# Second layer's values with tokens on the partitions, two head pairs to a group, in a fused two-block transformer kernel

## The reference

```python
proj = x @ w_in                       # 2048 x 7680
aq, ak, av, ag, bq, bk, bv, bg, cu, cglu, cg = jnp.split(proj, IN_OFFSETS, axis=-1)
# a: 4 heads, differential attention: softmax(q1 k1) - lam * softmax(q2 k2), halves of 64
ya = diff_attention(aq, ak, av, ...) * jax.nn.silu(ag)
# b: 8 heads of 128, three dilated window patterns merged
yb = dilated_attention(bq, bk, bv, ...) * jax.nn.silu(bg)
# c: 512 channels, GLU, causal depthwise conv of 31 taps, layer norm, swish, pointwise
yc = conformer_conv(cu, cglu, ...) * jax.nn.silu(cg)
x = layer_norm(ALPHA * x + jnp.concatenate([ya, yb, yc], -1) @ w_out, ln_g, ln_b)
```

## Time and profile before

| | |
|---|---|
| time, median of 3 runs | 2912.65 us (2910.31 to 2913.6) |
| the profiled execution's own time | 2911.83 us |
| its span | 2910.0 us |
| TensorE busy | 2887.2 us, 99% of the span |
| VectorE, ScalarE, GpSimd busy | 71%, 47%, 14% |
| granted TensorE clock, mean | 0.999 of full speed |
| `dil`, `diffa`, `diffb` of the first layer | about 2024.8 to 2327.4 us of the span |
| the same of the second layer | about 2501.4 to 2803.9 us |

### The profile page before, as it was taken

One profiled execution on the slowest core, in us unless ns is written; L12 is line 12 of the kernel. 1 busy time (PEld: TensorE's weight loads), 2 busy tenths in 40 slices (PEclk: granted clock), 3 DMA queues, 4 the chain that ended last, 5 costly groups with the idle time before them and its releaser, 6 DMA issues.

```text
span 2910.0 us, 43427 instructions
## 1 busy us (share of the span) xinstructions
PE 2887.2 (99%) x16142; PEld 2498.9 (86%) x16142; DVE 2071.8 (71%) x2314; ACT 1362.9 (47%) x1618; POOL 419.0 (14%) x392
## 2 busy tenths in 40 slices
PE   9999999999999999999999999999999999999999
PEld 7888888888888888888888888888888888888887
DVE  6666667875687677765666667876887856788766
ACT  6554544346654444443343344544344545444453
POOL 1000000204020000000000000013950100891010
PEclk9999999999999999999999999999999999999999
DMA  6555565654465666666555565566555555555455
GB/s 217 174 173 166 159 186 186 210 159 143 126 195 188 187 199 202 189 190 192 174 180 188 188 194 185 175 194 192 168 174 165 159 194 153 175 174 173 157 177 174
DMA packets 479573, 520.58 MB, mean 179 GB/s; under 512 B 17720, under 2 KB 438699, under 8 KB 479176
## 3 DMA queue, kind: packets, MB, share of 16 engines
q1 hardware_dynamic: 474528, 509.68, 55.8%
q0 software_dynamic: 4080, 6.30, 0.8%
q10 hardware_dynamic: 824, 2.69, 0.3%
HBM read 516.49 MB, written 2.12 MB: 178 GB/s over the span
## 4 chain that ended last, share of the span: by engine, by line
PE 63%; DVE 6%; ACT 3%; issue 2%; DMA 0%; DVEq 0%; ACTq 0%; SPq 0%
PE PG L2104 37%; PE PG L2107 18%; DVE WL L1266 2%; PE PG L2136 2%; PE PG L2138 2%; PE PG L2137 2%; ACT WH L650 1%; DVE G L1279 1%; DVE G L1583 0%; DVE MIX L1700 0%; PE PX L2168 0%; PE PX L2320 0%; PE PX L2221 0%; PE PX L2157 0%; DMA RAW<-in_w_in_dram 0%
## 5 line engine op out<-in xcount | busy, mean ns | idle before, releaser
L1266 DVE TENSOR_TENSOR WL<-RAW,WH 128x1024 fp32r<-128x1024 f32 (+1 forms) x956 | 1150.4, 1232 | 501.6 <-ACT WH L650 488.0
L650 ACT ACTIVATE WH<-RAW 128x1024 fp32r<-128x1024 f32 (+1 forms) x972 | 997.8, 1050 | 786.8 <-PE PG L2107 456.5
L2104 PE MATMUL PG<-XH,WH 128*128 128x512 f32 x4096 | 1295.8, 398 | 8.3 <-DVE WL L1266 4.4
L2107 PEld LDWEIGHTS PG<-XH,WL 128*128 128x128 f32 x4096 | 770.2, 188 | 182.1
L2107 PE MATMUL PG<-XH,WL 128*128 128x256 f32 x4096 | 805.7, 278 | 0.0
L2104 PE MATMUL PG<-YH,WH 128*128 128x512 f32 x2336 | 736.0, 396 | 1.9 <-DVE WL L1266 1.9
L2104 PEld LDWEIGHTS PG<-XH,WH 128*128 128x128 f32 x4096 | 625.8, 189 | 15.2 <-issue 9.4
L2107 PEld LDWEIGHTS PG<-YH,WL 128*128 128x128 f32 x2336 | 438.8, 188 | 103.7
L2107 PE MATMUL PG<-YH,WL 128*128 128x256 f32 x2336 | 459.0, 278 | 0.0
L2104 PEld LDWEIGHTS PG<-YH,WH 128*128 128x128 f32 x2336 | 355.9, 189 | 5.3 <-issue 3.4
L1279 DVE TENSOR_REDUCE G<-PG 128x512 f32<-128x1024 f32 x174 | 212.0, 1218 | 33.9 <-PE PG L2107 33.8
(11 more groups left out here) (302 smaller groups left out, 2092.0 us busy)
## 6 DMA issues: line engine op xcount, KB each, us to landing
RAW<-in_w_in_dram SPq DMA_DIRECT2D x488, 512.0 KB, 4.6
RAW<-in_w_ffn_gu_dram SPq DMA_DIRECT2D x176, 512.0 KB, 4.6
RAW<-in_w_ffn_down_dram SPq DMA_DIRECT2D x88, 512.0 KB, 4.7
RAW<-in_w_out_dram SPq DMA_DIRECT2D x64, 512.0 KB, 4.6
RAW<-in_w_rnn_out_dram SPq DMA_DIRECT2D x40, 512.0 KB, 4.6
RAW<-in_w_attn_out_dram SPq DMA_DIRECT2D x32, 512.0 KB, 4.8
RAW<-in_w_o_dram SPq DMA_DIRECT2D x32, 512.0 KB, 4.8
RAW<-in_w_ple_gate_dram SPq DMA_DIRECT2D x32, 512.0 KB, 5.1
```

The source lines that it names most:

```text
L650: nc.scalar.activation(WH[:, u % SLOTS, 0:nk, :], RAW[:, u % SLOTS, 0:nk, :], ACT.Copy)\
L1266: V_.tensor_tensor(WL[:, u % SLOTS, 0:nk, :], RAW[:, u % SLOTS, 0:nk, :], WH[:, u % SLOTS, 0:nk, :].bitcast(fp), ALU.subtract).then_inc(s. ...
L2104: mm(PG[:, 2 * par + j, :], WH[:, slot, kk, P * j:P * j + P], x, start=grp.opens and n == 0 and kk == 0, stop=False)
L2107: last = mm(PG[:, 2 * par + j, T:2 * T], WL[:, slot, kk, P * j:P * j + P], x[:, 0:T], start=False, stop=grp.closes and n == len(units) - 1 ...
```

## The change

The values of the second block are computed by wide groups with tokens on the partitions: one wide group of 512 columns carries the values of two head pairs, so `dil` has two (one for each two pairs) and `diffa` has one, which also serves `diffb`. The four transposes of the values and their copy from PSUM are gone; VectorE copies the wide group's result from PSUM to V (`values`), and V moves to another part of SBUF. The loop over the pairs in `dil` is written out as two halves of seven groups (q, k, v wide, gate, q, k, gate). The order of the work is written out by hand for `dil` and `diffa` on all engines: `take(g, n)` splits a group's units up to n, `give(g, n)` splits the first n units of a coming group early. TensorE's attention steps now stand inside groups (a dictionary gives the unit after which each comes). In `diffb` the values group is gone, the gate follows the second half of the pointwise product, the scores stand after the gate's second unit, and the probabilities' transposes after the second unit of `outa`.

```diff
-        V = F[:, 2048:2560].rearrange("p (a n) -> p a n", a=4)
+        V = AL[:, 20 * 2 * T:22 * 2 * T].rearrange("p (b n) -> p b n", b=NB)
...
+            def part(o, m, wide=False, pool=()):
+                return Group(w2, DC, A0 + 512 * o + COLS * m, 0, XH, wide=wide, pool=pool)
-            phases.append(Phase(f"dil{l}", 4, [Group(w2, DC, B0 + 1024 * o, COLS, XH) for o in range(4)]))
+            dil = []
+            for i in range(2):
+                a, b = ([Group(w2, DC, B0 + 1024 * o + COLS * pair_, 0, XH) for o in (0, 1, 3)]
+                        for pair_ in (2 * i, 2 * i + 1))
+                v = Group(w2, DC, B0 + 2048 + 2 * COLS * i, 0, XH, wide=True)
+                dil += [a[0], a[1], v, a[2]] + b
+            phases.append(Phase(f"dil{l}", 1, dil))
+            phases.append(Phase(f"diffa{l}", 1, [part(0, 0), part(1, 0), part(2, 0, wide=True), part(3, 0)]))
+            phases.append(Phase(f"diffb{l}", 1, [part(0, 1), pw[0], part(1, 1), pw[1], part(3, 1, pool=range(4))],
...
-                    split_next(f"diffb{l}", 5, 1)
                     diff_high(0)
-                elif j == 4:
-                    evacuated()
+                    give([p for p in phases if p.name == f"outa{l}"][0].body[0], 2)
                     soft(4)
                 else:
...
-                V_.tensor_copy(V, PX[:, 2, :].rearrange("p (a n) -> p a n", a=4))
...
+            def values(grp):
+
+                par = c.n.get("group", 0) % 2
+                dve.wait_ge(s.unit, c.next("seen", grp.seen))
+                V_.tensor_copy(V, PG[:, 2 * par:2 * par + 2, :]).then_inc(s.evac, 1)
+                c.add("group")
+                dve.wait_ge(s.evac, c.value("group"))
+            def take(grp, n):
+                split(grp, slice(ahead[0], n))
+                ahead[0] = 0
+
+            def give(grp, n):
+                split(grp, slice(0, n))
+                ahead[0] = n
...
+            def dil(body, before, following, l):
+                for i in range(2):
+                    q0, k0, v, g0, q1, k1, g1 = body[7 * i:7 * i + 7]
+                    take(q0, 4)
+                    if i:
+                        gate(body[6])
+                        taps(7, 1, l)
+                        give(k0, 2)
+                        transposed()
+                    else:
+                        for job in before:
+                            job()
+                    take(k0, 4)
+                    evacuate(q0, two(QR[:, 0, :]))
+                    taps(8 * i, 1, l)
+                    give(v, 2)
+                    if i:
+                        dil_out(1)
+                    take(v, 4)
+                    evacuate(k0, two(QR[:, 1, :]))
+                    taps(8 * i + 1, 2, l)
+                    split(v, slice(4, 8))
+                    dil_softmax(2 * i)
+                    take(g0, 4)
+                    values(v)
+                    transposed()
+                    take(q1, 4)
+                    gate(g0)
+                    dil_out(2 * i)
+                    taps(8 * i + 3, 1, l)
+                    take(k1, 4)
+                    evacuate(q1, two(QR[:, 0, :]))
+                    taps(8 * i + 4, 1, l)
+                    take(g1, 4)
+                    evacuate(k1, two(QR[:, 1, :]))
+                    taps(8 * i + 5, 2, l)
+                    give(body[7] if i == 0 else following, 2)
+                    dil_softmax(2 * i + 1)
...
+            def diffa(body, last_gate, l):
+                q, k, v, g = body
+                take(q, 4)
+                gate(last_gate)
+                taps(15, 1, l)
+                give(k, 2)
+                transposed()
+                take(k, 4)
+                evacuate(q, two(QR[:, 0, :]))
+                give(v, 2)
+                dil_out(3)
+                dve.wait_ge(s.sum, c.next("sum"))
...
+                take(v, 4)
+                evacuate(k, two(QR[:, 1, :]))
+                split(v, slice(4, 6))
+                inverse_root(PN[:, 0:T], PN[:, T:2 * T], NW, sums_read)
...
+                split(v, slice(6, 8))
+                give(g, 1)
+                diff_softmax(0, l, lambda: give_more(g, 3))
+                take(g, 4)
+                values(v)
+                transposed()
...
-                        split_next(f"diffb{l}", 5, 1)
                         diff_out(0, l)
+                        give([p for p in phases if p.name == f"outa{l}"][0].body[0], 2)
+                        diff_softmax(1, l)
...
-                v_transposes(c.n["group"] % 2).then_inc(s.turned, 1)
+                        last = nc.tensor.transpose(PX[:, h, to:to + P], x[:, frm:frm + P], IDENT)
...
+            def z_dil():
+                pe.wait_ge(s.evac, c.value("group"))
+                z_soft(1)
+            def in_dil(n):
+                i, what = divmod(n, 7)
+                return {0: {2: lambda: pt_soft(1)} if i else None,
+                        1: {2: lambda: heads_out(1)} if i else None,
+                        2: {3: z_dil, 7: lambda: pt_soft(1)},
+                        3: {3: lambda: heads_out(0)},
+                        6: {2: z_dil}}.get(what)
+            def conv_sums():
+                heads_out(1)
+                pe.wait_ge(s.conv, c.next("conv"))
+                for ch in range(CONVC):
+                    last = sum_features(0, CA[:, ch, :], ch == 0, ch == CONVC - 1)
+                last.then_inc(s.sum, 1)
+            def conv_squares():
+                squares_in()
+                for ch in range(CONVC):
+                    last = sum_features(1, SC_SQ[:, ch, :], ch == 0, ch == CONVC - 1)
+                last.then_inc(s.sumsq, 1)
+            def z_diffa():
+                pe.wait_ge(s.evac, c.value("group"))
+                ready()
+                z_soft(2)
+            def in_diffa(n):
+                return ({2: lambda: pt_soft(1)}, {2: conv_sums}, {1: conv_squares, 4: z_diffa},
+                        {1: lambda: pt_soft(2)})[n]
+            def z_diffb():
                 pe.wait_ge(s.evac, c.value("group", -1))
+                pe.wait_ge(s.op, c.value("op", 2))
+                z_soft(2)
...
+                        elif grp.wide and ph.name[:3] != "out":
+                            rows_group(grp, (), mid)
...
-                                mid = {0: diff_sum, 1: lambda: turn_x(0)} if j == 1 else None
+                                mid = ({1: lambda: pt_soft(2)}, {0: diff_sum, 1: lambda: turn_x(0)}, None, None)[j]
```

More of the change, by code:

```diff
@@ new lines, in diffa_gate @@
+            def diffa_gate():
+                silu_gate()
+                from_dve()
+                nc.scalar.activation(SC_SQ, CA, ACT.Tanh, scale=0.5).then_inc(s.act, 1)
+                act.wait_ge(s.act, c.next("act"))
+                from_dve()
+                for q in range(2):
+                    nc.scalar.activation(hi2(YH, q, base=DC), CA[:, 2 * q:2 * q + 2, :], ACT.Copy, scale=0.5)\
+                        .then_inc(s.act, 1)
+                    act.wait_ge(s.act, c.next("act"))
@@ L1768, in diff_softmax, with take @@
                 dve.wait_ge(s.ready, c.next("ready"))
-            def post_dil(grp, i, j, l):
-                if j == 0:
-                    evacuate(grp, two(QR[:, 0, :]))
-                    if not (isinstance(i, int) and i == 0):
-                        gated()
-                        low(YH, i - 1, two(OA), base=4)
-                elif j == 1:
-                    evacuate(grp, two(QR[:, 1, :]))
-                elif j == 2:
-                    evacuate(grp)
-                    dve.wait_ge(s.scores2, c.next("scores2"))
-                    scores(2, QSCALE, lambda x: 2 * i + (4 + x))
-                    inverse_sums(2)
-                    for h in range(2):
-                        for b, (lo, up) in enumerate(((0, P), (P, 3 * P))):
-                            x = S4[:, h, lo:up]
-                            ins = V_.tensor_scalar(x, x, der(D_RED + 16 + 2 * h + b), None, ALU.mult)
-                    ins.then_inc(s.ready, 1)
-                    dve.wait_ge(s.ready, c.next("ready"))
-                else:
-                    gate(grp)
-                at, m = ((0, 1), (1, 2), (3, 0), (3, 1))[j]
-                taps(4 * i + at, m, l)
+            def take(grp, n):
+                split(grp, slice(ahead[0], n))
+                ahead[0] = 0
@@ new lines, in give, with dil_softmax @@
+            def give(grp, n):
+                split(grp, slice(0, n))
+                ahead[0] = n
+            def dil_softmax(pair_):
+                dve.wait_ge(s.scores2, c.next("scores2"))
+                scores(2, QSCALE, lambda x: 2 * pair_ + (4 + x))
+                inverse_sums(2)
+                for h in range(2):
+                    for b, (lo, up) in enumerate(((0, P), (P, 3 * P))):
+                        x = S4[:, h, lo:up]
+                        ins = V_.tensor_scalar(x, x, der(D_RED + 16 + 2 * h + b), None, ALU.mult)
+                ins.then_inc(s.ready, 1)
```

(1 more changed line is left out.)

246 lines of the change are left out of this document (115 added, 131 removed).

## The result

The changed kernel takes 2920.91 us (median of 8 runs, 2918.15 to 2921.92) against 2911.99 of the kernel before on the same chip (8 runs, 2910.31 to 2913.6). The ratio is 1.003, 95% interval 1.002 to 1.0039: 8.9 us more. The forecast was 2915.4, within 0.2% of no change; slower by more than that, which had a chance of 0.28, is what came. The measured time is 0.1 us inside the upper end of the range (2921) and is rival B's case. The profiled execution has a span of 2919.2 us against 2910.0, 9.2 more. In what follows "before" and "after" are the two kernels. The ratios leave out one execution of the kernel of experiment 1, which took 5566 us at a granted clock of 0.909.

The account below looks back on a forecast made before the run. TensorE, busy for 99% of the span, was taken as the bound. New waits less its saved work, 2 x (2.0 + 3.2) - 7.6 = +2.8 us, gave 2915.4 us, no change; range 2904 to 2921.

Parts of the forecast that it names:

- rival B: Slower: GpSimd's WL units lock VectorE out in `diffb`, TensorE waits 5.9 us in `outa`; 2919.9 us, chance 0.24.
- What TensorE is spared: Transposes of the values 4.3 us (upper end 5.3) and wide instead of narrow groups 3.3 us, together 7.6 us.
- Rival C: The wide form saves nothing in the first block's attention, so 3.3 us are missing: 2918.7 us, chance 0.08.
- VectorE's copy of the values: Six copies of 128x1024 from PSUM replace twelve reductions; 1.2 us each, costed at nothing because off TensorE's path.
- Walk 1: Middle of `dil`: VectorE, slowed by GpSimd's taps, makes TensorE wait 1.0 and 1.7 us; +2.0 us a layer.
- Walk 2: `diffa`: scores, softmax, transposes come about 0.9 us late, as before; cost 0, between -0.9 and +0.9.
- Walk 3: `diffb` into `outa`: late softmax with one held output op, TensorE waits 3.7 us against 0.5; +3.2 us a layer.

Follow-up runs that it names:

- experiment 1: Changed kernel with VectorE splitting the two first units of k before its four taps in the second half of `dil`: 2915.34 us, ratio 1.0009.
- experiment 6: Changed kernel with four transposes of a constant put back behind each pair's six on TensorE, 48 in all, without VectorE's copy: 2922.37 us, ratio 1.0037.
- experiment 8: The version with both reorderings (experiment 7) plus the 48 transposes of a constant put back on TensorE: 2907.37 us, ratio 0.9983.
- experiment 2: Changed kernel with GpSimd's 15 conv taps cut from 256 to 8 columns, the opening tap left whole: 2914.05 us, ratio 1.0008.
- experiment 3: Changed kernel with GpSimd's four WL units of the last gate in each layer cut to 8 columns: 2910.47 us, ratio 0.9996.
- experiment 4: Changed kernel with the softmax right after the pointwise product and the first pair's output behind `outa`'s third to sixth unit: 2908.84 us, ratio 0.999.
- experiment 10: The version with both reorderings (experiment 7), GpSimd making WL for two units of the second differential gate instead of four, VectorE the others: 2910.86 us, ratio 0.9997.
- experiment 7: Changed kernel with both reorderings, k's units before the taps (experiment 1) and the output behind `outa`'s splits (experiment 4): 2904.45 us, ratio 0.9975.
- experiment 9: The unchanged program of experiment 7, with both reorderings, profiled once more: span 2901.6 us, time 2903.36 us.

## Why the prediction was right in its places and too small in one

**What TensorE is spared** held. The scores and a wide group of 96 matmuls fill 2047.44 to 2070.60 in after; matmuls start 0.228 us apart, 21.9 us a group where 21.76 was predicted. The four transposes are worth 0.44 us (1.01 less 0.57), the prediction's upper end, and not the 0.36 it took. That makes 5.3 + 2.6 = 7.9 us instead of 7.6. Rival C fell. This is work by the rows; as time the 48 transposes showed 1.5 us in experiment 6 and 2.9 in experiment 8.

**VectorE's copy of the values**: its rows stand at 1.22 us each, the value that was taken. No wait of TensorE from 2020 to 2345 ends with it.

**Walk 1** held: 2.85 us where 2.7 was predicted, at the two places named, by contention with GpSimd's taps (experiment 2). That the sum came so close is in part luck: the two waits are 0.49 and 2.36 us where 1.0 and 1.7 were predicted. **Walk 2** held within its bounds: the wait in `diffa` went from 0.92 to 0.41 us.

**Walk 3** is the step that failed, by its size. "I take one held op, as the row shows": three were held, product, low part and first output op, 3.9 us in place of 2.1. The wait became 4.8 us by the profile, 5.0 with the usual distance, where 3.7 less the third unit's 0.4 was expected. The row of before showed one held op because GpSimd's first unit began only at 2309.96 there, when product, low part and first op were under way or through the earlier trace rows; the walk itself said that three units now fall in that stretch, and didn't draw the conclusion. That is rival B, shown by experiment 3 (its mechanism alone) and experiment 4 (its place in the queue). The Trainium skill ("SBUF — State Buffer", "Who interferes with whom") has the rule by which all three are held; the trace of after agrees with it (1.30, 2.00 and 2.73 us).

**The missing term** is the clock: 2.7 us a layer behind the wait, in no case of the prediction. The Trainium skill ("TensorE: Matmul & The Clock Gate", "Part 1: The HAM clock gate") has a clock that falls when TensorE idles; the traces agree: it is at 0.50 behind the wait of 4.8 us and at 0.68 from 2317 to 2322 behind the one of 2.5 (experiment 10). The same part of the Trainium skill says that the moment at which the clock rises in a stream of matmuls differs from run to run; no run here was made to show that. That its fall differs, experiments 7 and 9 show.

**Rival B's time** came out within 1.0 us (2919.9 against 2920.9), and that is luck too. Its mechanism is the one that ran, but its wait in `outa` was 5.9 us where 5.0 was measured, and the clock's 2.7 was in no term.

**The sum with measured terms**, a layer: `dil` 2.85 - 0.7, `diffa` -0.5, the end of `diffb` -0.5, the wait in `outa` +5.0, the clock +2.7, which is +8.85; less TensorE's 7.9/2 it is +4.9, against 9.2/2 = 4.6 in the spans. The 0.3 left over stays open.

## What to carry to other kernels

- When GpSimd's work is placed beside another stretch, take every VectorE op with two SBUF inputs that starts beside a GpSimd op of two SBUF inputs as held until that one ends, as three were in after and one in the earlier trace rows, unless a row of this very stretch shows otherwise (the one that had started before GpSimd did, at 2309.55 in the earlier trace rows, took its usual 0.75 us); then look whether these ops stand ahead of something that TensorE waits for. Moving the output's operations and two splits behind it was worth 12 us here; giving two of GpSimd's four units back to VectorE made the version with both reorderings 6 us slower.
- A saving on the bounding engine is lost in a wait whose end another engine's own queue sets, like the one in `dil`. It isn't lost in a wait whose end hangs on the bounding engine's own result: `outa`'s stayed 4.83 us long and moved as a whole (experiment 6). Here the 7.9 us saved showed as time only once the two waits had been reordered away, and then 7.2 of them net (2904.45 against 2911.6).
- A wait of some microseconds on TensorE should be priced with the clock behind it, here more than half as much again (2.7 on 5.0).

## What was not expected of the hardware

The granted clock is at 0.50 behind a single wait of 4.83 us and is back 5.6 us after TensorE resumes. When TensorE resumed 1.6 us later (experiment 6), the clock came back at about the same time, so the loss was smaller. Shorter waits in the layer norm (0.8 and 1.8 us, about 4 us apart) let it fall in one execution of a program (experiment 7: 0.89 and 0.77 over two stretches of 5 us) and not in another (experiment 9), nor in the profiled executions of before, after and experiment 8, which have the same waits. That makes 5 x 0.11 + 5 x 0.23 = 1.7 us between executions of the same kernel.
